# Expert choice from 50 candidate pairs, and the gate's factor in the other one-hot by ScalarE

## What is computed

```python
q = (h @ w_pq).reshape(T, HEADS, 2, 128)                 # 8 heads
sub = einsum('thpc,hpnc->thpn', q, keys)                 # 128 scores for each half key
s_top, i_top = top_k(sub, 16)                            # 16 best of each half
cand_s = s_top[:, :, 0, :, None] + s_top[:, :, 1, None, :]   # 16 x 16 sums
best_s, pos = top_k(cand_s, 16)                          # 16 best pairs
expert = 128 * i_top[.. first ..] + i_top[.. second ..]  # of those pairs
gate = softmax(best_s)
u = peer_u[expert]; act = gelu(x . u)                    # 128 experts per token
out = sum(gate * act * peer_v[expert])
```

## Time and profile before

| | us |
|---|---|
| median of 3 runs | 2258.17 (2255.44 to 2262.65) |
| the profiled execution, its own time | 2260.75 |
| its span | 2258.9 |
| TensorE busy | 2170.7 |
| VectorE busy | 1596.9 |
| ScalarE busy | 1186.8 |
| GpSimd busy | 182.4 |

### The profile page before, as it was taken

The page is one execution under the profiler, slowest core; times in us unless marked ns, Lnnn a source line. Parts: engine busy times, 40 slices in busy tenths (PEclk is TensorE's granted clock), DMA queues, the critical chain, the costliest instruction groups (busy, mean ns, idle before and its releaser), DMA issues.

```text
span 2258.9 us, 38897 instructions
## 1 busy us (share of the span) xinstructions
PE 2170.7 (96%) x15108; PEld 1998.4 (88%) x15108; DVE 1596.9 (71%) x3201; ACT 1186.8 (53%) x2115; POOL 182.4 (8%) x228
## 2 busy tenths in 40 slices
PE   7999899999999999999998998999999999999998
PEld 5988899999999888888887988999999998888886
DVE  3455668797999768888755445597979997555555
ACT  3455544445777554444554444444457775554554
POOL 0000001313222000000000000013132220000000
PEclk9999999999999999999998998999999999999999
DMA  8655455555333467778542434555553334566664
GB/s 330 215 202 174 176 183 182 186 184 162 122 131 123 153 224 276 278 280 288 197 160 97 137 104 135 183 187 186 182 165 131 121 124 149 183 192 194 195 194 132
DMA packets 110550, 407.57 MB, mean 180 GB/s; under 512 B 11552, under 2 KB 11936, under 8 KB 110112
## 3 DMA queue, kind: packets, MB, share of 16 engines
q1 hardware_dynamic: 98928, 361.81, 48.1%
q10 hardware_dynamic: 11440, 43.28, 5.0%
HBM read 403.99 MB, written 1.05 MB: 179 GB/s over the span
## 4 chain that ended last, share of the span: by engine, by line
PE 83%; DVE 7%; ACT 3%; issue 3%; POOL 2%; DMA 1%; DVEq 0%; ACTq 0%; SPq 0%
PE PB L428 24%; PE PB L430 24%; PE PB L429 24%; PE PB L796 4%; POOL AR L2191 2%; ACT WH L1079 2%; DVE WL L1520 1%; DVE OH L1906 1%; PE PB L495 1%; PE PB L474 1%; PE PB L766 1%; DVE OH L1903 1%; PE PB L1051 1%; DVE AR L1849 1%; DVE AR L1841 1%
## 5 line engine op out<-in xcount | busy, mean ns | idle before, releaser
L1520 DVE TENSOR_TENSOR WL<-RING,WH 128x1024 fp32r<-128x1024 f32 x651 | 802.8, 1235 | 514.4 <-ACT WH L1079 512.9
L1079 ACT ACTIVATE WH<-RING 128x1024 fp32r<-128x1024 f32 x651 | 686.6, 1056 | 476.8 <-PE PB L430 474.4
L428 PE MATMUL PB<-HH,WH 128*128 128x256 f32 x2848 | 823.6, 289 | 16.0 <-DVE WL L1520 9.2
L430 PE MATMUL PB<-HH,WL 128*128 128x256 f32 x2848 | 808.0, 284 | 0.0
L429 PE MATMUL PB<-HL,WH 128*128 128x256 f32 x2848 | 807.7, 284 | 0.0
L428 PEld LDWEIGHTS PB<-HH,WH 128*128 128x128 f32 x2848 | 548.6, 193 | 23.4 <-issue 16.7
L429 PEld LDWEIGHTS PB<-HL,WH 128*128 128x128 f32 x2848 | 548.4, 193 | 0.2
L430 PEld LDWEIGHTS PB<-HH,WL 128*128 128x128 f32 x2848 | 547.6, 192 | 0.0
L428 PE MATMUL PB<-WH,HH 128*128 128x512 f32 (+2 forms) x1344 | 497.8, 370 | 21.9 <-DVE AR L1524 6.8
L430 PE MATMUL PB<-WH,HL 128*128 128x512 f32 (+2 forms) x1344 | 493.6, 367 | 0.0
L429 PE MATMUL PB<-WL,HH 128*128 128x512 f32 (+2 forms) x1344 | 493.3, 367 | 0.0
(11 more groups left out here) (219 smaller groups left out, 1557.0 us busy)
## 6 DMA issues: line engine op xcount, KB each, us to landing
RING<-in_u SPq DMA_DIRECT2D x256, 512.0 KB, 3.3
RING<-in_v SPq DMA_DIRECT2D x256, 512.0 KB, 4.2
RING<-in_win SPq DMA_DIRECT2D x90, 512.0 KB, 3.2
AR<-in_wm ACTq DMA_DIRECT2D x40, 1024.0 KB, 6.3
RING<-in_wq SPq DMA_DIRECT2D x32, 512.0 KB, 3.3
AR<-in_wm SPq DMA_DIRECT2D x8, 1024.0 KB, 16.3
RING<-in_wout SPq DMA_DIRECT2D x16, 512.0 KB, 3.3
RING<-in_sk SPq DMA_DIRECT2D x8, 512.0 KB, 3.2
```

The lines of the kernel that those rows point to most:

```text
L428: e.matmul(o, ah, bh, start=start, stop=False)
L430: return e.matmul(o, al, bh, start=False, stop=stop)
L1079: e.activation(hi(t), raw(("w", t), words(t)), ACT.Copy).then_inc(s_hi, 1)
L1520: e.tensor_tensor(lo(t), raw(("w", t), words(t)), hi(t).bitcast(F32), ALU.subtract).then_inc(s_lo, 1)
```

## The change

It does two things.

First, the candidates. If both lists are sorted, the pair (i, j) can be among the 16 best only if (i + 1)(j + 1) <= 16. These are 50 pairs: row i has 16 // (i + 1) of them, and starts at PAIR0[i]. GpSimd forms these 50 sums per head with 9 additions, over all heads at once, in place of 8 additions of 256 sums. VectorE's searches run over 50 columns. Since a position is no longer 16 i + j, the row is found by adding up steps: TA holds 64 x (first number) + PAIR0, TB its differences, with 2^23 added to the first, and the sum of TB over all rows whose start is not above the position gives both the first number and the row's start as bits (VectorE shifts and masks them out). The compares, products and sums over 2048 columns are done in two halves, and the steps per token half fall from 49 to 40; `choose_steps` gives two steps in every twelfth tile instead of every fourth. The copies of the transposed numbers become a function `chosen`, called in tile 78. A copy of minus the gate is added there (MR).

Second, the one-hots. The gate is the factor of the first one-hot, not of the second. ScalarE computes relu(gate - gate x |iota - number|), token by token, as four operations with scale and bias from MR and GIT. VectorE makes the second one-hot by one compare over 512 columns. Each third quad VectorE makes the first one too, as compare and product. GpSimd and its two semaphores are out of the gate stage.

```diff
 def choose_steps(j):
-    return 0 if j >= JG else 2 if j % 4 == 3 else 1
+    return 0 if j >= JG else 2 if j % 12 == 11 else 1
+CHOSEN = {28: 0, 68: 1}
...
     # ScalarE, one_hots
-                    if q % 4 == 0:
+                    if q % 3 == 0:
                         return
...
-                    own.done(n)
-                    e.activation(OH[:, i, 0, :, :], OH[:, i, 0, :, :], ACT.Relu, scale=-1.0, bias=1.0).then_inc(s_oa, 1)
+                    for t in range(4):
+                        c = slice(4 * q + t, 4 * q + t + 1)
+                        own.done(ns[t])
+                        r = e.activation(OH[:, i, 0, t, :], OH[:, i, 0, t, :], ACT.Relu, scale=MR[:, 0, c],
+                                         bias=GIT[:, 0, c])
+                    r.then_inc(s_oa, 1)
...
     # VectorE, one_hots
-                    e.tensor_tensor(OH[:, i, 1, 0:2, :], io[:, 0:2, :], bc(2, 2), ALU.is_equal).then_inc(s_oe, 1)
-                    for t in (2, 3):
-                        c = 4 * q + t
-                        r = e.tensor_scalar(OH[:, i, 1, t, :], iota, GIT[:, 2, c:c + 1], GIT[:, 0, c:c + 1],
-                                            ALU.is_equal, ALU.mult)
-                    if q % 4 == 0:
-                        r = e.tensor_tensor(OH[:, i, 0, :, :], io, bc(1, 4), ALU.is_equal)
+                    if q % 3 == 0:
+                        n = own.mark(e.tensor_tensor(OH[:, i, 0, :, :], io, bc(1, 4), ALU.is_equal))
+                    r = e.tensor_tensor(OH[:, i, 1, :, :], io, bc(2, 4), ALU.is_equal)
+                    if q % 3 == 0:
+                        own.done(n)
+                        r = e.tensor_tensor(OH[:, i, 0, :, :], OH[:, i, 0, :, :], bc(0, 4), ALU.mult)
                     r.then_inc(s_ov, 1)
...
     # VectorE, choose: after the 16 best of each half key
+                    own.done(own.mark(e.scalar_tensor_tensor(out=TA, in0=ff[:, :, 0, :], scalar=64.0,
+                                                             in1=pair0.unsqueeze(1).to_broadcast([128, 8, 16]),
+                                                             op0=ALU.mult, op1=ALU.add)))
+                    e.tensor_scalar(TB[:, :, 0:1], TA[:, :, 0:1], 8388608.0, None, ALU.add)
+                    e.tensor_tensor(TB[:, :, 1:16], TA[:, :, 1:16], TA[:, :, 0:15], ALU.subtract)
...
     # VectorE, choose: the numbers, now in halves m
+                        for m in range(2):
+                            hk = slice(64 * m, 64 * m + 64)
+                            row = iota[:, 0:16] if s else pair0
+                            e.tensor_tensor(EQ[:, hk, :], ABF[:, a, s, hk].unsqueeze(2).to_broadcast([128, 64, 16]),
+                                            row.unsqueeze(1).to_broadcast([128, 64, 16]),
+                                            ALU.is_equal if s else ALU.is_ge).then_inc(s_eq, 1)
+                            yield
...
     # GpSimd
-                for q in range(NQ):
-                    o = OH[:, q % 2, 1, 0:2, :]
-                    e.wait_ge(s_oe, 64 * blk + q + 1)
-                    e.tensor_tensor(o, o, GIT[:, 0, 4 * q:4 * q + 2].unsqueeze(2).to_broadcast([128, 2, 128]),
-                                    ALU.mult).then_inc(s_op, 1)
```

More of the change, by code:

```diff
@@ L31 @@
 N_SMALL = 168
+PAIRS = [16 // (i + 1) for i in range(16)]
+PAIR0 = [sum(PAIRS[:i]) for i in range(16)]
+N_PAIR = sum(PAIRS)
 K_ID, K_ONE, K_IOTA, N_KC = 0, 128, 256, 384
@@ L1322, in one_hots @@
                         e.wait_ge(s_gp, 64 * blk + q - 1)
+                    ns = []
                     for t in range(4):
-                        n = own.mark(e.activation(OH[:, i, 0, t, :], iota, ACT.Abs, scale=-1.0,
-                                                  bias=GIT[:, 1, 4 * q + t:4 * q + t + 1]))
-                    own.done(n)
-                    e.activation(OH[:, i, 0, :, :], OH[:, i, 0, :, :], ACT.Relu, scale=-1.0, bias=1.0).then_inc(s_oa, 1)
+                        ns.append(own.mark(e.activation(OH[:, i, 0, t, :], iota, ACT.Abs, scale=-1.0,
+                                                        bias=GIT[:, 1, 4 * q + t:4 * q + t + 1])))
+                    for t in range(4):
[4 more added lines that the diff above has]
+                    r.then_inc(s_oa, 1)
                 for j in range(NK):
@@ L1332, in peer @@
                         step += 1
-                        if step in (36, 85):
-                            a = step // 50
+                        if step in CHOSEN:
+                            a = CHOSEN[step]
                             g = GI[:, 0, a, :].rearrange("p (h k) -> p h k", h=8)
@@ L1825, in choose @@
                     e.tensor_tensor(g, ts, ts[:, :, 0:1].to_broadcast([128, 8, 16]), ALU.subtract).then_inc(s_ge, 1)
[L1826 to L1830, removed]
+                    t_ab = own.mark(e.tensor_copy(ABF[:, a, 0, :], PO[:, a, :, :].rearrange("p h k -> p (h k)")))
                     yield
@@ L1836, in choose @@
                     own.done(n)
-                    t_g = own.mark(e.tensor_tensor(g, g, rc.unsqueeze(2).to_broadcast([128, 8, 16]), ALU.mult))
+                    e.tensor_tensor(g, g, rc.unsqueeze(2).to_broadcast([128, 8, 16]), ALU.mult)
                     yield
@@ new lines, in choose @@
+                        yield
+                        dst = GI[:, 2, a, :] if s else ABF[:, a, 1, :]
+                        for m in range(2):
+                            hk = slice(64 * m, 64 * m + 64)
+                            e.wait_ge(s_em, 8 * blk + 4 * a + 2 * s + m + 1)
+                            r = e.tensor_reduce(dst[:, hk], EQ[:, hk, :], AX, ALU.add)
+                            if m == 0:
+                                yield
+                                yield
+                        if s:
+                            r.then_inc(s_gi, 1)
+                            yield
+                            continue
@@ new lines, in choose @@
+                        own.done(own.mark(r))
+                        bits = ABF[:, a, 1, :].bitcast(U32)
+                        yield
+                        e.tensor_scalar(AB[:, a, 0, :], bits, 6, 127, ALU.logical_shift_right, ALU.bitwise_and)
+                        own.done(own.mark(e.tensor_scalar(AB[:, a, 1, :], bits, 63, None, ALU.bitwise_and)))
+                        own.done(own.mark(e.tensor_copy(GI[:, 1:3, a, :], AB[:, a, :, :])))
+                        own.done(own.mark(e.tensor_tensor(ABF[:, a, 1, :], ABF[:, a, 0, :], GI[:, 2, a, :], ALU.subtract)))
@@ L1858, in choose, with chosen @@
+            def chosen(blk):
                 for s in range(3):
                     e.wait_ge(s_gtr, 3 * blk + s + 1)
[L1860 removed]
+                    r = e.tensor_copy(GIT[:, s, :], PB[4 + s][:, 0:256])
+                    if s == 0:
+                        r = e.tensor_scalar(MR[:, 0, :], PB[4][:, 0:256], -1.0, None, ALU.mult)
+                    r.then_inc(s_git, 1)
             chunk_sum = [0]
@@ L2177, in peer @@
                     ff = IF[:, a, :, :].rearrange("p (h s) k -> p h s k", s=2)
+                    if a == 0:
+                        if blk:
+                            e.wait_ge(s_rope, 6)
+                        for i in range(16):
+                            r = e.memset(pair0[:, i:i + 1], float(PAIR0[i]))
+                        r.then_inc(s_pair, 1)
                     e.wait_ge(s_topv, 2 * blk + a + 1)
```

64 lines of the change are left out of this document (27 added, 37 removed).

## The result

The changed kernel takes 2271.74 us in the median of 5 runs (2270.6 to 2279.89), the kernel before 2258.17 in 5 (2255.44 to 2262.65). The ratio is 1.0068, with a 95% interval of 1.0056 to 1.008: slower by 0.7%, 13.6 us. The forecast was 2278, with 2246 to 2292 as the range. The profiled execution took 2270.6 us with a span of 2268.7.

A forecast was written before the change was run, and what follows sets the result against it. TensorE, 96% busy, was taken to bound the kernel, so only its weight-load waits counted. 2260.75 + 30.2 at the gates - 10.0 in the choice = 2281.0, less 2.58 gives 2278 us, range 2246 to 2292.

The forecast's parts named there:

- The bound and what could be won: TensorE's weight-load waits in gate and choice stages: removing all, 8.0 + 4.9 us per block, would bring 25.8 us.
- ScalarE's step: Gate stage: four Abs and four narrow Relus of 0.49 us take 2.86 us to their end, where it was 1.93.
- The prediction's aside: Gate stage: by the skill page's 93 ns charges ScalarE would end after 2.8 us, moving the sum by under 1 us.
- VectorE's three operations: Gate stage, every third quad: two compares and a product on VectorE take 0.60 + 0.60 + 0.68 = 1.88 us.
- The walk: Gate stage, waits by quad over a 12-quad pattern: 4.33 us together, 23.1 per block against 8.0, +30.2 for both blocks.
- (a): Gate stage paced by VectorE's total, so all 16 us of L796 waits go; 2232 us, chance 0.22 including a mixed case.
- (b): Gate stage: the Relu's second operand is free, ScalarE's step is 2.46 us; 2263 us, chance 0.13.
- (c): Choice stage: VectorE's wait for second scores breaks its cover, at most 2.87 us per block; 2284 us, within the forecast's 0.65.
- (d): Choice stage keeps its stalls because GpSimd's products hold up VectorE's low parts; 2288 us, within the forecast's 0.65.
- The signs: Gate stage: L796 waits near 23 us, ended equally by Relu and VectorE's product; ScalarE near 87% busy, VectorE below 90%.
- The choice: Choice stage: waits for expert tiles, transposes and part of the first quad's go, a gain of 2 x (3.2 + 1.2 + 0.6) = 10.0 us.
- The sum: Whole kernel: 2260.75 + 30.2 - 10.0 = 2281.0 us, less 2.58 gives 2278 us on the median's scale.

The follow-up runs named there:

- e7_choice_dve_first: Kernel before with the choice from 50 pairs, and VectorE making each tile's first-slot one-hots ahead of its low part; 2235.19 us, ratio 0.9895.
- e3_wide: Changed kernel with ScalarE's one wide Relu over 512 columns again, gate factor left out in two quads of three; 2248.58 us, ratio 0.9952.
- e3_narrow: Changed kernel with constant scale and bias in ScalarE's four narrow Relus, gate factor left out in two quads of three; 2249.22 us, ratio 0.9954.
- e1_choice: Kernel before with only the choice from 50 pairs; its one-hots, waits and GpSimd products kept; 2247.62 us, ratio 0.9955.
- e8_pool_product: Kernel before with choice from 50 pairs, wide Relu without factor, VectorE's first slots early, GpSimd multiplying all four second one-hots by gates; 2233.43 us, ratio 0.9892.

## Why the prediction was right, point by point

**The bound and what could be won.** Waits of TensorE's weight load were the only thing to win. `e7_choice_dve_first` shows nearly the whole of it: of the 12.9 us that the prediction counted in a block it keeps 0.2, so 25.4 of the 25.8 are gone by the waits. By the medians it is 22 us below the kernel before, with its runs at a granted clock of 0.984 to 0.986 where most of that kernel's are at 0.988.

**ScalarE's step.** Expected 0.49 us for a narrow Relu with two operands and 2.86 for the whole step. Measured 487 ns, and one step of the changed kernel, 652.78 to 655.60, is 2.82:

```profile
652.78 1.27 ACT L1335 ACTIVATE OH<-KC,GIT 128x128 f32<-128x128 f32 x4
653.95 1.65 ACT L1341 ACTIVATE OH<-OH,GIT,MR 128x128 f32<-128x128 f32 x4
...
655.71 0.97 PEld L806 LDWEIGHTS PB<-OH 128*128 128x128 f32 x8 [0.30 <-DVE AR L1954]
```

The prediction's aside that a step of 2.8 us would move the sum by under 1 us is too small by its own walk: some 0.05 us off each of three waits, twice 64/12 times, is over 1.5 us. The weight load follows the end by 0.11 us. Here too the row names VectorE's L1954 as the releaser, which had ended at 655.44; ScalarE's end fits.

**VectorE's three operations.** Expected 1.88 us, measured 1.89 from 640.78 to 642.67:

```profile
640.78 0.68 DVE L1940 TENSOR_TENSOR OH<-KC,GIT 128x512 f32<-128x512 f32 x1
...
641.98 0.69 DVE L1944 TENSOR_TENSOR OH<-OH,GIT 128x512 f32<-128x512 f32 x1
```

**The walk.** The weight loads of the quads 3 to 11 of one turn in the changed kernel, those that waited:

```profile
642.78 0.97 PEld L806 LDWEIGHTS PB<-OH 128*128 128x128 f32 x8 [1.26 <-issue]
652.31 0.97 PEld L806 LDWEIGHTS PB<-OH 128*128 128x128 f32 x8 [0.33 <-issue]
...
662.80 0.97 PEld L806 LDWEIGHTS PB<-OH 128*128 128x128 f32 x8 [0.93 <-issue]
669.64 0.97 PEld L806 LDWEIGHTS PB<-OH 128*128 128x128 f32 x8 [0.69 <-DVE AR L1954]
```

With the 0.30 at 655.71 these are q mod 12 = 3, 6, 7, 9 and 11:

| q mod 12 | expected | measured |
|---|---|---|
| 2 | 0.18 | 0 |
| 3 | 1.33 | 1.26 |
| 6 | 0.52 | 0.33 |
| 7 | 0.37 | 0.30 |
| 9 | 1.04 | 0.93 |
| 11 | 0.89 | 0.69 |
| sum | 4.33 | 3.51 |

The mechanism was right in five of six places, and the wait at q = 2 didn't come. The largest part of the difference is one term: the lag from the end of a one-hot to the weight load. I took 0.2 from the earlier trace rows (0.23 there); in the changed kernel it is 0.11, behind ScalarE and behind VectorE (the product of q = 3 ended at 642.67). That is 0.09 us for each of six waits, at most 0.5 of the 0.8, and so at most 6 of the 8.6 us of both blocks; it is less where a wait that gets shorter lets the next one grow, as q = 7 behind q = 6. What makes up the rest was not parted. Why the lag is shorter was not tried either. At the first quad of the kernel before it is 0.11 too (VectorE's L1909 ended at 555.71, the weight load began at 555.82), behind a tensor_tensor operation and with fewer engines to wait for; the 0.23 stands behind L1906, with one engine more than in the changed kernel. Either would fit, and no run shows which.

**The rivals.** (a) would have needed VectorE's total to be the bound. It fell by 15% in the gate stage and the waits more than doubled; and in `e7_choice_dve_first` VectorE is busier than ever (175.7 of 180) with no wait. VectorE's load was not the bound in any of these kernels. Its condition, ScalarE within 1.97 us, was placed a little too low: with steps of 1.9 (`e3_wide`) and also of 2.07 (`e3_narrow`, 650.63 to 652.70) no quad of ScalarE's is late. With the lag of 0.11 for 0.2 the same sum gives 2.06. (b) falls by the 487 ns. (c) had its cover: VectorE waits for the second scores, and TensorE for nothing:

```profile
431.56 0.30 DVE L1802 MAX8 AR<-PB 128x8 f32<-128x128 f32 x1 [4.15 <-PE PB L777]
```

It waits 4.15 us, less than the 7.5 that I gave. (d) didn't happen.

**The signs.** ScalarE is 84% busy in the gate stage (near 87 expected), VectorE 80% (below 90), and the waits of L806 are 18.8 us (near 23). They were to end in like parts by ScalarE's Relu and VectorE's product. They don't: by the table above ScalarE's quads have 0.99 us of the 3.51, and VectorE's 2.52. The prediction's own walk had said the same, 1.44 of 4.33.

**The choice.** 4.8 us of waits per block went, 5.0 were expected, and `e1_choice` shows 10.0 us for both blocks by itself in the medians (9.6 by these waits), the term of the sum; that it fits to the tenth is chance. One thing in it went otherwise than told. GpSimd's products took longer, not the same:

```profile
397.04 10.49 POOL L2236 TENSOR_TENSOR AR<-AR 128x256 f32<-128x256 f32 x8 [30.57 <-DVE AR L1865]
```

Eight took 10.49 us where the earlier trace rows have 8.52: five of the eight were held up by an operation of VectorE's, where before it was three (how, see below). Three of the halves' sums waited for them, 3.3 us together, and the time between the steps covered it. The search over 50 columns takes 206 ns (L1836, against 419 in the earlier trace rows).

**The sum.** Forecast +20.2 us, measured +13.6: 2 x 15.1 expected at the gates and 2 x 10.8 measured there make 8.6 of difference by the waits. The choice gave 2 x 4.8 for 2 x 5.0, 0.4 less, so the waits alone would say +12.0, and 1.6 us that no listed wait shows make it 13.6. That the forecast is 6.6 us off and not 8.6 is luck: these two small terms happen to go the other way.

## What to carry to other kernels

When several engines build one operand for TensorE, ask for the length of each engine's step between two fixed points of the chain, not for its busy share: taking 15% of the load off the busiest engine made this stage slower, since a step of 1.9 us on the other became 2.8 where some 2.06 was the limit, and since every third quad now had three operations in a row (1.89 us, where the late quad of before had 1.23) behind the low part on the engine that was relieved on average. A multiplication that looks free as the scale and bias of an operation must be priced with its form: here per-token factors forced four narrow instructions with two operands each. And an in-order engine's queue is part of the chain: putting urgent work ahead of work that waits for another engine gave 12 us in the medians and 16 in the waits (`e1_choice` to `e7_choice_dve_first`), while doing so on both engines at once only moved the wait.

## What the runs showed of the hardware

- Operands from memory on ScalarE: 300, 395 and 487 ns for 128 columns with none, one and two, and successive ones start 0.20, 0.29 and 0.39 us apart.
- VectorE and GpSimd hold each other up when both work on two-input operations, and they take turns. GpSimd's eight products from 397.04 us last either 0.75 us (three) or 1.65 to 1.74 (five), nothing between; each long one began while VectorE was in an operation on 1024 columns with two inputs, and ended 0.59 to 0.61 us after the end of that. In turn the four such operations of VectorE's that began during a product (1.51 to 1.76 us long) each ended 1.07 or 1.08 us after the end of the product. VectorE's sum at 403.76, with one input, kept its 1.21 us, and so did the product beside it its 0.75. VectorE's compare of 1024 columns beside GpSimd's products took 1.76 us, alone 1.22; the low part up to 2.06 beside a product of 512 columns (`e8_pool_product`), alone 1.22. GpSimd's product of 256 columns took 1.06 us on average in the earlier trace rows, and 1.31 here (10.49 for eight).
- The runs of one kernel differ with the granted clock: 2270.6 us at a mean of 0.989, 2275.5 at 0.986 and 2279.9 at 0.983, all of the changed kernel. Between 1100 and 1440 us, where the blocks meet and TensorE rests often, the profiles show 0.93 to 0.96, and 1.00 in the windows of the gate stage. What was compared here by waits is not touched by it.
